# RWKV-7 chunk inverse in four groups with the transposed product merged, alternating heads, rates ahead of decays

## The chip, the cores and the metric

One core of a Trainium2 chip runs the whole program. The metric is the device time of one execution in microseconds; the kernel before takes 2446.75 us (median of 3 runs, 2444.73 to 2447.14).

## What is computed

A diffusion backbone of two layers over 256 context tokens and 256 latent tokens of width 1024. Layer 0 is a Hyena long convolution and a dense SwiGLU; layer 1 is a bidirectional RWKV-7 time mixing and a top-2-of-8 expert SwiGLU. The change touches the RWKV-7 mixer, whose recurrence the reference writes as a scan over tokens, for 16 heads of width 64 and two directions:

```python
def step(S, inp):
    r_t, w_t, k_t, v_t, a_t, b_t = inp
    sa = jnp.einsum('bhvk,bhk->bhv', S, a_t)
    S = S * w_t[:, :, None, :] + sa[..., None] * b_t[:, :, None, :] + v_t[..., None] * k_t[:, :, None, :]
    return S, jnp.einsum('bhvk,bhk->bhv', S, r_t)
```

## The kernel before, in words

**Stages.** The program is one long list of instructions for each engine, kept in order by semaphores: Hyena and the dense SwiGLU to about 784 us of the profiled span, a preparation of RWKV to 850 us, eight pairs of heads to about 1380 us, then the experts. Each pair of heads is one call of `pair(i, more)` on PE, ACT, DVE and POOL, written out eight times; SP loads the next pair's weights.

**One pair.** The 512 tokens are 8 chunks of 64, two to a block of 128 partitions, so NB = 4 blocks for each direction d, and 2 NB = 8 blocks x for each head h of the pair. Instead of a scan, each chunk is solved at once, which needs the inverse of a 64x64 unit triangular matrix for every head, direction and chunk. `scores` (L1350) makes the products of the keys; `first_join` on DVE puts the first ones into `TM`; then a hardware loop `Fori(0, LOOPED)` (L1392) of 4 levels doubles the inverted blocks inside 32x32 blocks, and `last_first` and `last_second` join the 32s to 64s. Every one of those products is a 32x32 tile, four of them in the four quarters of the array.

**One level of the loop,** with h = 0 and 1 as the two groups:
- PE `level_first(h)` (L1297): waits for `level_turned`, multiplies `AB` by `TN` (the blocks of `TM`, transposed) into bank h.
- ACT `first_copy` (L2033): copies bank h to `YP`, 128x256.
- PE `level_second(h)` (L1306): waits for `level_copied`, multiplies `YP` by `TM` into bank 2 + h.
- DVE `join` (L2791): merges the new entries from bank 2 + h into `TM` under a mask of bits, 128x256; `turn_level` (L2774) then transposes `TM` into `TN`, and only then is `level_turned` raised.

The counts that PE waits for inside the loop are registers, `lv * 2 + constant`. `settle` (L659) raises a counter that nobody in this stage waits for; it marks for the program where earlier work is done, and rides on the wait instruction before it.

**Ahead work.** While pair i is being solved, the projections of pair i + 1 are made. PE: `ahead_keys` (L1235 to 1237), `ahead_decay` (L1248, waits for ACT's copy of the keys because it uses their bank), `ahead_rate` (L1256). ACT: `ahead_rates` does the two decay sigmoids (L1992) and then the two rate sigmoids (L1996). DVE: `ahead_scan` (L2705, L2708) needs the decay sigmoids, then `ahead_rate` (L2713 to 2722), then the pair's own `m_ready` (L2831), `n_ready` (L2838), `g_ready` (L2844) and the first states (L2849). PE's `ahead_values` (L1271) may start only when `n_ready_1` is done, because it writes the bank that `n_ready` reads.

**Order of the small products.** The 64x64 products of `scores` (L1350), the third scores (L1370), and the later sums (L1441, L1452, L1463, L1473) go through one head and then the other. The program's float32 product appears as two MATMUL records and two LDWEIGHTS records.

## Time and profile before

| | us |
|---|---|
| median of 3 runs | 2446.75 (2444.73 to 2447.14) |
| the profiled execution, its own time | 2449.69 |
| its span | 2447.9 |
| PE busy | 2349.8 (96%), 24762 matmuls |
| DVE busy | 1600.3 (65%) |
| ACT busy | 1267.7 (52%) |
| granted TensorE clock, mean | 0.982 of full |
| the eight pairs of heads, about 850 to 1380 us | 530 |

How it is read: the slices of the page show PE nearly full everywhere, but busy time of overlapping small matmuls says little about how close they follow each other. So the pairs are read from the order of time: the starts of groups of records on one engine, the idle time ahead of them, and what ended it. "issue" is idle time for which the profile has no releaser.

### The profile page before, as it was taken

Reading aid. Unit: us, or ns where it says so; the run is one execution under the profiler, and the core shown is the slowest. Engines: PE = TensorE matmul, PEld = TensorE weight load, DVE = VectorE, ACT = ScalarE, POOL = GpSimd, SP = SyncE. Lnnn points to the kernel's source line nnn. Section 1 sums busy time; section 2 is a strip of 40 time slices with the busy share of each in tenths; the row PEclk is TensorE's granted clock in tenths of the full one; section 3 lists DMA queues with packets and bytes.
Section 4 is the critical chain, followed back from the end, with each engine's and each line's share of the span. In section 5 each row is a group of like instructions: output and inputs, shape, how many; then the busy total and the mean of one; then the engine's idle time right before and its main releaser. Section 6 shows DMA issues by size and latency. Waiting matters only on the chain.

```text
span 2447.9 us, 57064 instructions
## 1 busy us (share of the span) xinstructions
PE 2349.8 (96%) x24762; PEld 1909.6 (78%) x24762; DVE 1600.3 (65%) x1808; ACT 1267.7 (52%) x1400; POOL 233.4 (10%) x212
## 2 busy tenths in 40 slices
PE   8999999999999899889988989999999999999998
PEld 4677676888886477777776778888888888888887
DVE  2544876222324946555565378888888888888887
ACT  4322025222222844444444277777777777777774
POOL 2000642000000332211111100000000000000000
PEclk8999999999999899999999999999999999999999
DMA  7566126332324201111111479999999999999993
GB/s 268 188 224 241 52 87 172 86 103 86 103 86 142 80 21 32 32 31 32 31 32 44 146 272 368 334 369 333 370 335 369 336 366 337 365 339 361 344 362 134
DMA packets 249079, 490.41 MB, mean 200 GB/s; under 512 B 14615, under 2 KB 107567, under 8 KB 248623
## 3 DMA queue, kind: packets, MB, share of 16 engines
q1 hardware_dynamic: 247214, 481.31, 55.5%
q10 hardware_dynamic: 1730, 7.10, 0.8%
q8 instruction: 109, 1.79, 0.3%
q14 instruction: 26, 0.21, 0.0%
HBM read 486.29 MB, written 2.10 MB: 200 GB/s over the span
## 4 chain that ended last, share of the span: by engine, by line
PE 92%; DVE 3%; issue 2%; ACT 1%; DMA 1%; SPq 0%; POOL 0%; DVEq 0%; ACTq 0%
PE bank L1621 26%; PE bank L1648 12%; PE bank L1157 3%; PE bank L1158 3%; PE bank L1159 3%; PE bank L1271 2%; PE bank L1297 2%; PE bank L1034 2%; PE bank L1063 2%; PE bank L1035 2%; PE bank L1036 2%; PE bank L1175 2%; PE bank L1174 2%; PE bank L1176 2%; PE bank L1306 1%
## 5 line engine op out<-in xcount | busy, mean ns | idle before, releaser
L2966 DVE TENSOR_TENSOR w_low<-expert_w,w_high 128x1792 fp32r<-128x1792 f32 (+2 forms) x384 | 769.0, 2023 | 125.3 <-ACT w_high L2165 123.7
L2165 ACT CAST w_high<-expert_w 128x1792 fp32r<-128x1792 f32 (+2 forms) x384 | 652.9, 1701 | 247.0 <-PE bank L1621 154.3
L1621 PE MATMUL bank<-w_high,xg_high 128*128 128x448 f32 x1024 | 294.2, 369 | 4.0 <-DVE xg_low L2956 4.0
L1621 PE MATMUL bank<-w_low,xg_high 128*128 128x448 f32 x1024 | 291.7, 366 | 0.0
L1621 PE MATMUL bank<-w_high,xg_low 128*128 128x448 f32 x1024 | 291.5, 366 | 0.0
L1621 PEld LDWEIGHTS bank<-w_high,xg_high 128*128 128x128 f32 x1024 | 191.3, 189 | 20.1 <-DVE xg_low L2956 4.1
L1621 PEld LDWEIGHTS bank<-w_low,xg_high 128*128 128x128 f32 x1024 | 193.2, 189 | 15.5
L1621 PEld LDWEIGHTS bank<-w_high,xg_low 128*128 128x128 f32 x1024 | 192.9, 188 | 15.4
L1648 PE MATMUL bank<-w_high,hid_high 128*128 128x512 f32 x448 | 175.3, 391 | 0.0
L1648 PE MATMUL bank<-w_high,hid_low 128*128 128x512 f32 x448 | 174.5, 389 | 0.0
L1648 PE MATMUL bank<-w_low,hid_high 128*128 128x512 f32 x448 | 174.3, 389 | 0.0
L1157 PE MATMUL bank<-u_high,ring_high 128*128 128x512 f32 x352 | 139.2, 395 | 2.1 <-DVE u_low L2616 1.6
L1158 PE MATMUL bank<-u_low,ring_high 128*128 128x512 f32 x352 | 138.9, 395 | 0.0
L1159 PE MATMUL bank<-u_high,ring_low 128*128 128x512 f32 x352 | 138.4, 393 | 0.0
L2635 DVE TENSOR_TENSOR arena<-arena,bank 128x512 f32 (+1 forms) x22 | 15.1, 687 | 127.5 <-ACT arena L1927 127.5
L1648 PEld LDWEIGHTS bank<-w_high,hid_low 128*128 128x128 f32 x448 | 84.1, 188 | 17.8
L1648 PEld LDWEIGHTS bank<-w_low,hid_high 128*128 128x128 f32 x448 | 84.1, 188 | 16.7
L1648 PEld LDWEIGHTS bank<-w_high,hid_high 128*128 128x128 f32 x448 | 84.1, 188 | 16.6
L1927 ACT ACTIVATE arena<-bank 128x512 f32<-128x512 f32 x22 | 13.2, 598 | 158.9 <-PE bank L1159 158.9
L2791 DVE COPY_PREDICATED arena<-arena,bank 128x256 f32<-128x256 int32 x64 | 27.5, 430 | 84.8 <-PE bank L1306 84.8
L1157 PEld LDWEIGHTS bank<-u_high,ring_high 128*128 128x128 f32 x352 | 66.5, 189 | 18.2 <-issue 3.0
L2033 ACT COPY arena<-bank 128x256 f32<-128x256 f32 x80 | 29.4, 383 | 96.8 <-PE bank L1297 96.4
(426 smaller groups left out, 4200.5 us busy)
## 6 DMA issues: line engine op xcount, KB each, us to landing
expert_w<-in_moe_w_dram SPq DMA_DIRECT2D x192, 1792.0 KB, 9.4
arena<-in_mod_w_dram SPq DMA_DIRECT2D x48, 1024.0 KB, 8.1
arena<-in_ffn_w_dram SPq DMA_DIRECT2D x44, 512.0 KB, 5.2
arena<-in_hy_w_in_dram SPq DMA_DIRECT2D x12, 1024.0 KB, 5.2
arena<-in_rw_w_rkv_dram SPq DMA_DIRECT2D x48, 256.0 KB, 2.8
arena<-in_ffn_w_dram SPq DMA_DIRECT2D x11, 1024.0 KB, 4.9
arena<-in_hy_w_out_dram SPq DMA_DIRECT2D x4, 1024.0 KB, 9.2
arena<-in_rw_w_out_dram SPq DMA_DIRECT2D x8, 512.0 KB, 3.4
```

The lines of the kernel that those rows point to most:

```text
L1034: pe.matmul(bank[m % 4][:, :], wh[:, k, :], uh, start=(k == 0), stop=False)
L1035: pe.matmul(bank[m % 4][:, :], wh[:, k, :], ul, start=False, stop=False)
L1036: last = pe.matmul(bank[m % 4][:, :], wl[:, k, :], uh, start=False, stop=(k == KT - 1))
L1063: last = pe.matmul(bank[2 * part + f][:, :], fwd[:, tt, (2 * part + f) * P:(2 * part + f + 1) * P], ZT[:, 2 * s + tt, half * 512:half * 51 ...
L1157: pe.matmul(bank[b + h][:, :], wh[:, c, :], uh, start=(k == 0), stop=False)
L1158: pe.matmul(bank[b + h][:, :], wh[:, c, :], ul, start=False, stop=False)
L1159: last = pe.matmul(bank[b + h][:, :], wl[:, c, :], uh, start=False, stop=(k == KT - 1))
L1174: pe.matmul(bank[m][:, :], wh[:, o, :], hh, start=first, stop=False)
L1621: last = pe.matmul(bank[b0 + v][:, 0:EH], x[:, k, :], w_[:, kk, v * EH:v * EH + EH], start=(k == 0 and x is XGH and w_ is wh), stop=(k == ...
L1648: last = pe.matmul(bank[4 + half][:, :], x[:, f, :], w_[:, f - 4 * i_, :], start=(c == 0 and f == 0 and x is HTH and w_ is wh), stop=(c == ...
L2165: act.copy(high_piece(kind, n), piece(kind, ering[q % ERN], n // 2, n % 2))\
L2966: dve.tensor_tensor(piece(kind, low[s], n // 2, n % 2), piece(kind, ering[s], n // 2, n % 2), high_piece(kind, n).bitcast(F32), ALU.subtract)\
```

## The change

- **Four groups.** The levels run over (h, d), one head in one direction, 4 blocks each. Both products of a group go to the same bank, 2h + d. ACT's copies and DVE's joins become 128x128 and twice as many.
- **Merged transposed.** `level_second` swaps its operands, so that it gives the transposed product; `join` merges it straight into `TN` (the bits of the masks are stored the other way round), and raises `level_ready`. Behind the four joins `turn_back` transposes `TN` into `TM` and raises `level_turned`.
- **Waits in the loop.** `level_first` waits for `level_ready`. `level_second` waits for `level_turned` and `level_copied`, whose counts now differ (READY is 20 a pair, COPIED 18).
- **Rates ahead of decays** on PE and ACT; DVE's order stays.
- **Heads alternate** in the 64x64 products; the sums at L1441 wait for the last copy of both heads at once.
- In the dense stage, a semaphore `u_whole` on DVE is replaced by the chain on which the next chained instruction waits.

```diff
-PER_PAIR = 2 * (LOOPED + 1)
+GROUPS = 4
+READY = GROUPS * (LOOPED + 1)
+COPIED = GROUPS * LOOPED + 2
+PRODUCTS = 2 * COPIED
 LD_KEYS, LD_LORA, LD_VALUES, LD_QUERIES, LD_PAIR = 32, 64, 96, 128, 160
 
 
...
-                          [near(b, a) for b in LEVELS for a in (True, False)] +
+                          [near(b, a) for b in LEVELS for a in (False, True)] +
                           [level(C // 2, False), level(C // 2, True)], 1)
     return (common.astype(np.float32), layer0.astype(np.float32), layer1.astype(np.float32),
...
-            return 2 * PER_PAIR * i + 4 * lv + 2 * half + h + 1
+            return PRODUCTS * i + 2 * GROUPS * lv + (GROUPS if lv < LOOPED else 2) * half + h + 1
 
         CHUNKS = [[0, 1, 2, 3, 4, 5, 6, 7], [3, 2, 1, 0, 7, 6, 5, 4]]
...
             def ahead_rate(j):
                 if isinstance(j, int) and j == 0:
                     pe.wait_ge(sem("gap_turned"), 2)
+                pe.wait_ge(sem("ld_pair"), j * LD_PAIR + LD_LORA)
                 step(pe, "pair_copies", "z_copy_1", j - 1)
                 for d in range(2):
...
 
-            def level_first(h, count):
-                pe.wait_ge(sem("level_turned"), count)
+            def level_first(h, d, ready):
+                pe.wait_ge(sem("level_ready"), ready)
                 settle(pe)
-                for x in range(2 * NB):
+                for x in range(d * NB, d * NB + NB):
                     for j in range(4):
                         q, cs = slice(HC * j, HC * j + HC), slice(HC * (j % 2), HC * (j % 2) + HC)
-                        last = mm(bank[h][q, x * HC:x * HC + HC], AB[h][q, x, cs], TN[h][q, x, :], start=True, stop=True)
+                        last = mm(bank[2 * h + d][q, x * HC:x * HC + HC], AB[h][q, x, cs], TN[h][q, x, :], start=True, stop=True)
                 last.then_inc(sem("level_products"), 1)
 
-            def level_second(h, count):
-                pe.wait_ge(sem("level_copied"), count)
+            def level_second(h, d, turned, copied):
+                pe.wait_ge(sem("level_turned"), turned)
+                pe.wait_ge(sem("level_copied"), copied)
                 settle(pe)
-                for x in range(2 * NB):
+                for x in range(d * NB, d * NB + NB):
                     for j in range(4):
                         q = slice(HC * j, HC * j + HC)
-                        last = mm(bank[2 + h][q, x * HC:x * HC + HC], YP[h][q, x, :], TM[h][q, x, :], start=True, stop=True)
+                        last = mm(bank[2 * h + d][q, x * HC:x * HC + HC], TM[h][q, x, :], YP[h][q, x, :], start=True, stop=True)
                 last.then_inc(sem("level_products"), 1)
 
             def last_first(h, i):
-                pe.wait_ge(sem("level_turned"), PER_PAIR * i + 2 * LOOPED + h + 1)
+                pe.wait_ge(sem("level_ready"), READY * i + GROUPS * LOOPED + 2 * h + 2)
                 settle(pe)
...
                 def scores(name, b0, left, right):
-                    for h in range(2):
-                        r = hd(h)
-                        for x in range(2 * NB):
-                            d, b = divmod(x, NB)
-                            for s_ in range(2):
-                                t = slice(b * P + s_ * C, b * P + s_ * C + C)
-                                last = mm(bank[b0 + h][hd(s_), x * C:x * C + C], left[d][r, t], right[d][r, t],
+                    for x in range(2 * NB):
+                        d, b = divmod(x, NB)
+                        for s_ in range(2):
+                            t = slice(b * P + s_ * C, b * P + s_ * C + C)
+                            for h in range(2):
+                                last = mm(bank[b0 + h][hd(s_), x * C:x * C + C], left[d][hd(h), t], right[d][hd(h), t],
                                           start=True, stop=True)
-                        last.then_inc(sem("pair_products"), one("pair_products", f"{name}_{h}"))
+                                if x == 2 * NB - 1 and s_ == 1:
+                                    last.then_inc(sem("pair_products"), one("pair_products", f"{name}_{h}"))
 
...
                     for h in range(2):
-                        level_first(h, lv * 2 + (PER_PAIR * i + h + 1))
+                        for d in range(2):
+                            level_first(h, d, lv * GROUPS + (READY * i + 2 * h + d + 1))
                     for h in range(2):
-                        level_second(h, lv * 2 + (PER_PAIR * i + h + 1))
+                        for d in range(2):
+                            level_second(h, d, lv * GROUPS + (READY * i + 2 * h + d + 1),
+                                         lv * GROUPS + (COPIED * i + 2 * h + d + 1))
                 step(pe, "pair_vectors", "out_masked_1", i)
                 for d in range(2):
...
                     .then_inc(sem("pair_products"), one("pair_products", "bonus_sum"))
                 if more:
                     ahead_keys(i + 1, range(KT))
+                    ahead_rate(i + 1)
                     ahead_decay(i + 1)
-                    ahead_rate(i + 1)
 
...
                     ahead_key_sum(i + 1)
-                for h in range(2):
-                    step(pe, "pair_copies", f"wu_copy_{h}1", i)
-                    settle(pe)
-                    for x in range(2 * NB):
-                        d, b = divmod(x, NB)
+                step(pe, "pair_copies", "wu_copy_11", i)
+                settle(pe)
+                for x in range(2 * NB):
+                    d, b = divmod(x, NB)
+                    for h in range(2):
                         for s_ in range(2):
                             last = mm(bank[4 + s_][hd(h), x * C:x * C + C], Q[hd(s_), 2 * h + d, b, 0:C],
                                       Btok[d][hd(s_), b, hd(h)], start=True, stop=True)
                 last.then_inc(sem("pair_products"), one("pair_products", "m_sum"))
...
                 for d in range(2):
+                    step(act, "ahead_products", f"rate_{d}", j)
+                    act.activation(AS[d], bank[6 + d][:, :], ACT.Sigmoid, bias=dcol("rw_a0", j + 8 * d))\
+                        .then_inc(sem("ahead_copies"), one("ahead_copies", f"rate_sig_{d}"))
+                for d in range(2):
                     step(act, "ahead_products", f"decay_{d}", j)
                     act.activation(SG[d], bank[4 + d][:, :], ACT.Sigmoid, bias=dcol("rw_w0", j + 8 * d))\
                         .then_inc(sem("ahead_copies"), one("ahead_copies", f"decay_sig_{d}"))
-                for d in range(2):
-                    step(act, "ahead_products", f"rate_{d}", j)
-                    act.activation(AS[d], bank[6 + d][:, :], ACT.Sigmoid, bias=dcol("rw_a0", j + 8 * d))\
-                        .then_inc(sem("ahead_copies"), one("ahead_copies", f"rate_sig_{d}"))
 
             def ahead_key_log(j):
...
 
-                def first_copy(lv, h):
-                    act.wait_ge(sem("level_products"), level_product(i, lv, 0, h))
-                    act.copy(YP[h].rearrange("p x c -> p (x c)"), bank[h][:, 0:2 * NB * HC]).then_inc(sem("level_copied"), 1)
+                def first_copy(lv, h, d):
+                    act.wait_ge(sem("level_products"), level_product(i, lv, 0, 2 * h + d))
+                    act.copy(YP[h][:, d * NB:d * NB + NB, :].rearrange("p x c -> p (x c)"), bank[2 * h + d][:, d * P:d * P + P])\
+                        .then_inc(sem("level_copied"), 1)
+
+                def last_copy(h):
+                    act.wait_ge(sem("level_products"), level_product(i, LOOPED, 0, h))
+                    act.copy(YP[h].rearrange("p x c -> p (x c)"), bank[2 * h][:, 0:2 * NB * HC]).then_inc(sem("level_copied"), 1)
 
                 def z_copy(h):
...
                                              per_stream(fold_shift[0], k, 1), ALU.mult, ALU.add)
-                last.then_inc(sem("u_whole"), 1)
+                link(last)
 
             def u_low(j):
                 dve.wait_ge(sem("u_high"), j + 1)
-                dve.wait_ge(sem("u_whole"), j + 1)
                 g, c = j // 2, 2 * (j % 2)
                 dve.tensor_tensor(UL[g][:, c:c + 2, :], UT[:, 2 * j:2 * j + 2, :], UH[g][:, c:c + 2, :].bitcast(F32),
...
 
-                def turn_level(h):
-                    dve.transpose(TN[h].rearrange("p b c -> p (b c)"), TM[h].rearrange("p b c -> p (b c)"))\
-                        .then_inc(sem("level_turned"), 1)
-
                 def first_join(h):
...
+                    dve.sem_inc(sem("level_turned"), 2)
+
+                def join(lv, h, d):
+                    dve.wait_ge(sem("level_products"), level_product(i, lv - 1, 1, 2 * h + d))
                     settle(dve)
-                    dve.copy_predicated(by_dir(TM[h], HC), each_block(level_bits[lv - 1]),
-                                        by_dir(bank[2 + h][:, 0:2 * NB * HC], HC))\
-                        .then_inc(sem("pair_vectors"), one("pair_vectors", f"joined_{lv}_{h}"))
-                    step(dve, "pair_vectors", f"joined_{lv}_{h}", i)
-                    turn_level(h)
+                    mask = level_bits[lv - 1][:, d, :].unsqueeze(1).to_broadcast([P, NB, HC])
+                    dve.copy_predicated(TN[h][:, d * NB:d * NB + NB, :], mask,
+                                        bank[2 * h + d][:, d * P:d * P + P].rearrange("p (b c) -> p b c", c=HC))\
+                        .then_inc(sem("level_ready"), 1)
+
+                def turn_back(lv, h, d):
+                    dve.wait_ge(sem("level_ready"), READY * i + GROUPS * lv + 2 * h + d + 1)
+                    part = slice(d * NB, d * NB + NB)
+                    dve.transpose(TM[h][:, part, :].rearrange("p b c -> p (b c)"), TN[h][:, part, :].rearrange("p b c -> p (b c)"))\
+                        .then_inc(sem("level_turned"), 1)
 
                 for h in range(2):
                     first_join(h)
@@ -2807,7 +2822,11 @@
                 dve.tensor_copy(DC, DCn).then_inc(sem("pair_vectors"), one("pair_vectors", "chunk_decay"))
                 for lv in range(1, LOOPED + 1):
                     for h in range(2):
-                        join(lv, h)
+                        for d in range(2):
+                            join(lv, h, d)
+                    for h in range(2):
+                        for d in range(2):
+                            turn_back(lv, h, d)
                 if i:
                     finish(i - 1)
...
```

## Rows read from the trace of the kernel before

**Rows 1.** windows: one pair each, then a stretch of a second level

```profile
core 0: us, PE busy (x) PEld busy (x) DVE busy (x) ACT busy (x) POOL busy (x), PEclk, DMA share, GB/s
986.24:1052.34 66.10, 59.79 (x1945) 47.25 (x1944) 37.92 (x76) 30.02 (x56) 12.59 (x12) 0.97 0.10 29
1253.00:1322.70 69.70, 60.88 (x1946) 47.55 (x1946) 38.20 (x76) 29.85 (x56) 12.57 (x12) 0.95 0.10 28
...
997.60:999.40 1.80, 1.72 (x126) 1.75 (x130) 0.70 (x2) 0.37 (x1) 0.00 (x0) 0.50 0.19 54
```

**Rows 2.** timeline of PE, loop of the third pair

```profile
start us, us, engine line op out<-in xcount [idle before <-releaser]
997.68 1.96 PE L1297 MATMUL bank<-arena 32*32 32x32 f32 x128 [0.57 <-DVE arena L2774]
...
1001.73 1.55 PE L1297 MATMUL bank<-arena 32*32 32x32 f32 x128 [0.66 <-DVE arena L2774]
...
1005.11 1.55 PE L1297 MATMUL bank<-arena 32*32 32x32 f32 x128 [0.52 <-DVE arena L2774]
```

**Rows 3.** timeline of DVE, third pair

```profile
991.37 1.27 DVE L2805 TENSOR_TENSOR arena<-bank,arena 128x512 f32<-128x512 f32 x2
...
1004.04 0.45 DVE L2791 COPY_PREDICATED arena<-arena,bank 128x256 f32<-128x256 int32 x1 [1.65 <-PE bank L1306]
1004.52 0.45 DVE L2774 STREAM_TRANSPOSE arena<-arena 128x256 f32<-128x256 f32 x1
```

**Rows 4.** PE's sequencer by source line, whole trace or one stretch

```profile
engine op xcount: duration ns min/median/max, first and last start us, forms
L1292 PEldq ALU_OP  x32: 36/36/36, 861.2 to 1342.1; - x32
...
L1392 PEldq COMPARE_BRANCH  x1: 208/208/208, 1004.4 to 1004.4; - x1
...
L659 PEldq EVENT_SEMAPHORE  x1: 51/51/51, 991.6 to 991.6; - x1
```

**Rows 5.** timeline of weight loads, fourth pair, then third

```profile
1058.66 0.64 PEld L1297 LDWEIGHTS bank<-arena 32*32 32x32 f32 x64 [0.17 <-issue]
...
1059.34 0.46 PEld L1297 LDWEIGHTS bank<-arena 32*32 32x32 f32 x40
...
1005.89 0.66 PEld L1297 LDWEIGHTS bank<-arena 32*32 32x32 f32 x64
...
1006.49 0.31 PEld L1306 LDWEIGHTS bank<-arena 32*32 32x32 f32 x25
```

**Rows 6.** ACT's copies of 128x128, by source line

```profile
L2083 ACT COPY arena<-bank x16: 266/269/273, 914.3 to 1376.5; 128x128 f32<-128x128 f32 x16
```

**Rows 7.** waits of PE, 850 to 1323 us

```profile
engine line waited for: us in total, times, longest us
PE bank L1306 <- issue: 16.8, 7, 2.8
PE bank L1297 <- DVE arena L2774: 8.8, 18, 0.7
PE bank L1248 <- ACT arena L1987: 5.4, 7, 0.8
```

**Rows 8.** page, DMA queues: packets, MB, share

```profile
q8 instruction: 109, 1.79, 0.3%
```

**Rows 9.** timeline of PE, 64x64 products, third pair

```profile
986.24 3.26 PE L1350 MATMUL bank<-arena 64*64 64x64 f32 x122
...
1029.83 1.96 PE L1452 MATMUL bank<-arena 64*64 64x64 f32 x118
```

**Rows 10.** timelines of ACT, DVE and PE, ahead work in the second pair

```profile
956.87 1.27 ACT L1992 ACTIVATE arena<-bank,arena 128x512 f32<-128x512 f32 x2
958.03 1.27 ACT L1996 ACTIVATE arena<-bank,arena 128x512 f32<-128x512 f32 x2
...
957.59 1.23 DVE L2705 TENSOR_TENSOR_SCAN arena<-arena 128x512 f32<-128x512 f32 x1 [1.51 <-ACT arena L1992]
...
966.64 1.28 DVE L2838 TENSOR_TENSOR arena<-bank,arena 128x512 f32<-128x512 f32 x2
...
968.71 1.98 PE L1271 MATMUL bank<-arena 128*128 128x512 f32 x4
```

**Rows 11.** timeline of PE, start of the first pair

```profile
850.23 5.69 PE L1350 MATMUL bank<-arena 64*64 64x64 f32 x122 [2.37 <-DVE arena L2743]
```

**Rows 12.** timeline of PE, dense stage

```profile
410.32 0.76 PE L1157 MATMUL bank<-u_high,ring_high 128*128 128x512 f32 x1 [1.58 <-DVE u_low L2616]
```

More of the change, by code:

```diff
@@ L1445, in pair @@
                     d, b = divmod(x, NB)
-                    for h in range(2):
-                        for part in range(2):
+                    for part in range(2):
+                        for h in range(2):
                             for s_ in range(2):
```

59 lines of the change are left out of this document (29 added, 30 removed).

## The prediction

> **What bounds the kernel now.** I read the windows of single pairs first, then the order of time of PE inside one pair, then DVE's, then what PE's sequencer issues between matmuls, and last the waits. The windows [rows 1] show one pair with PE recorded as busy for 59.8 of 66.1 us and DVE for 37.9: PE looks full. It isn't, in the sense that matters here. In the loop of levels a 32x32 MATMUL follows the one before it at 8.7 ns, while each is drawn much longer, so "busy" says nothing of the spacing; only the starts do. In the third pair the second, third and fourth level start at 997.68, 1001.73 and 1005.11 [rows 2]. So the second costs 4.05 us and a warm one 3.38; the fourth has the same body. PE waits for DVE ahead of these levels: 18 waits of at most 0.7 us, 8.8 us in total, for L2774 [rows 7]. DVE's row shows why: the join takes 0.45, the transposition of head 0 another 0.45, and only its end at 1004.97 lets PE begin at 1005.11 [rows 3].
>
> But behind this wait stands a second bound. PE's sequencer has work of its own at the turn of the loop: a compare-and-branch of 0.208 from 1004.4, and then a register operation and a wait instruction of 0.051 [rows 4]. From the last product of a level to the first of the next I take 0.52 for these, worked out as 0.05 ahead of the branch, its 0.21, 0.05 for the register, 0.05 for the wait, and 0.16 of steps between them and to the array. So without DVE a level would still be about 3.0, not less.
>
> **Cost of a switch between groups.** This decides the sum. In the weight loads of the fourth pair, head 0 ends at 1058.66 + 0.64 = 1059.30, head 1 starts at 1059.34; between them the sequencer computes a register (ALU_OP at L1292, 36 ns, once per iteration, 32 in all) and then waits. In the third pair, where L1306 follows L1297 and the count is in a register already, 1005.89 + 0.66 = 1006.55 and the next starts at 1006.49, ahead of that end [rows 4, 5]. The difference is 0.10. With the ends drawn in, the spacing is about 0.146 with a register to compute and 0.044 with a bare wait instruction: the sequencer leads the array by too little to hide either.
>
> **Part 1, the levels.** A new warm level issues the same 256 MATMUL (8 x 32 x 8.8 ns = 2.26 us) but switches group seven times, not three. What is computed: firsts wait for `lv * 4 + (20 i + ...)`, of which one comes with the loop's own operation, so three; seconds wait for `level_turned` with the same values and for `level_copied` with `lv * 4 + (18 i + ...)`, four values more where i is 2 or above. So seven switches at 0.146 = 1.02; plus 0.52 for the turn, and 0.02: 3.82 us, against 3.38. Does DVE or ACT bind instead? DVE's eight operations on 128x128 are about 0.28 each (half of 0.45 plus a fixed part, an estimate from [rows 3]), 2.2 us, and the join of group 0 is done long before the level ends; ACT's four copies are 0.27 each [rows 6]. Both are hidden, and so the transposition is indeed off the path. So the gain of the change (no wait for L2774) is real and smaller than what PE's own sequencer adds: +0.44 for a warm level; rounded, +0.4.
>
> Third and fourth level: i = 2 to 7, 6 x 0.8 = +4.8; i = 1, where two of the four values coincide, +0.4; i = 0, where both counts are equal and shared, 0. Sum +5.2. Second level: TensorE runs there at 0.50 of its clock, so 1.2 GHz, behind the stall [rows 1], its 128 MATMUL at L1297 take 1.96 instead of 1.55 [rows 2], the array is slower than the sequencer and hides the registers, while the 0.66 wait for DVE shrinks: -0.1 x 8 = -0.8. First level: a stall of issue bounds it (part 2), which swallows the registers: 0, and +0.4 each, 3.2 in all, if it didn't.
>
> **Part 2, the stalls.** PE waits seven times for "issue" ahead of L1306, 16.8 us, at most 2.8 [rows 7]. They stand where instructions run for the first time, and PE's queue of instructions moves 109 packets of 1.79 MB, so 16 KB each [rows 8]: I read them as waits for the program. A stretch of dense short matmuls spends a piece in less time than the next needs. Two things follow. Faster 64x64 products bring little, as they run into the same wait. And the length of a pair depends on where the pieces fall: pairs 1, 4 and 7 (counting from one) are about 3 us longer, compare 66.10 and 69.70 [rows 1]. The change drops a few instructions, so it shifts the phase. I take the number of long pairs as unchanged, and +-1 of them, 2.8 us, goes into the range. The Trainium skill says of this (Runtime: NRT & Kernel Launch, Instruction fetch mechanics) that blocks of 16 KiB are fetched ahead of use and the crossing is mostly hidden. By it the stalls would be something else and would not move; the row's 2.8 us at most isn't hidden, and I keep it.
>
> **Part 3, alternating heads.** `scores` (L1350) for head 0 and then head 1 takes 3.26 us for 122 recorded of 128 MATMUL, 26 ns each; L1452, whose neighbours already differ in rows and banks, takes 1.96 for 118 of 128, 16 ns [rows 9]. If the alternated ones get this, `scored_0` comes at the end of all 64 products instead of half way, 0.15 to 0.2 later (64 x 15 ns against 32 x 26), and the start of the levels hangs on DVE behind it (the masks at L2805 start at 991.37 and end about when PE enters [rows 3]). Against it stands a fetch gain of about 0.45 in half of the pairs. Net 0, with bounds of +0.2 and -0.5 a pair. In pair 8, without ahead work, the sums alternate too: -0.4. [...]
>
> **Part 4, rates ahead of decays.** Now in the second pair ACT's decay sigmoids (1.27 each) start at 956.87, the scan at 957.59, DVE runs without a pause to `n_ready_1` at 966.64 + 1.28 = 967.92, PE's L1271 starts 0.8 later at 968.71 [rows 10]. With rates first PE doesn't meet the wait for ACT's key copy at L1248, 5.4 us in seven waits [rows 7], and goes on to `wu` 0.8 earlier. The rates' own waits are no new ones: the loads' is the one that the decays had at this place, and `z_copy_1` is over when the keys are done. But the decays' copy is no earlier, and ACT makes two rate sigmoids first: the group of decays comes as late as the group of rates does now, 956.87 to 958.03, +1.15. Scan +1.15, everything behind it on DVE +1.15, L1271 at scan + 11.68 in terms of the old scan. It was at 11.12 here (957.59 to 968.71): +0.56. Over the seven pairs the old distance was 11.38, 11.12, 11.65, 10.98, 11.11, 11.04, 12.79: +0.30, +0.56, +0.03, +0.70, +0.57, +0.64, -1.11 = +1.7. From L1271 on the pair is constant. Before pair one PE already waits 2.37 for DVE [rows 11], the same chain is 1.15 later, nothing covers it: +1.15.
>
> **Part 5, `u_whole`.** One semaphore becomes the chain; a chained wait on DVE may delay `u_low`, on which L1157 waits 1.58 once [rows 12]: +0.3, bounds 0 and +1.
>
> **Sum.** 5.2 - 0.8 + 0 - 0.4 + 1.7 + 1.15 + 0.3 = +7.15 us. The profiled execution is 2449.7, the median 2446.75, 2.9 under it; the terms are differences, so they go onto the median: 2453.9.
>
> **Rivals.**
> R1, registers are hidden: a switch costs 0.044 whether or not a value is computed. Then a level is 2.26 + 7 x 0.044 + 0.52 = 3.1, -0.28 for each of 16 warm levels, -4.5 instead of +5.2 and the rest shrinks to: 2453.9 - 9.7 = 2444. For it: the sequencer's operations are only 36 ns long. Against: the 0.10 in [rows 5]. It decides at 0.083 a switch, where 3.38 is met. 0.20.
> R2, DVE isn't the chain in the ahead zone: PE keeps its 0.77 and the scan's delay vanishes in slack: about -0.8 x 7 instead of +1.7 and 1.15 less, 2453.9 - 8.5 = 2445.4. Against: DVE's unbroken row. 0.13.
> R3, the phase of the pieces: the three long pairs become like the others, -8.4, 2445.5; or one or two become long, 2456.7 to 2459.5. 0.12, the halves alike.
> R4, slower still: `level_second`'s two waits against registers don't fit in one instruction. 0.1 more at four switches, 0.4 x 16 warm levels = +6.4: 2460.3. For it: two register values at once, which no wait of the kernel before has. Against: one wait instruction already does two things, as L659's counter rides on it [rows 4]. 0.13.
> R5, the change doesn't do what it says: heads alternate, the products stay at 26 ns, `scored_0` is 0.75 later: with a third of it absorbed 0.5 x 8 = +4, 2458. 0.05, inside the range.
> The forecast and its near variants: 0.37.
>
> **How the numbers follow.** 0.2% is 4.9 us, about what a measurement of this kernel can tell from no change: faster is below 2441.9, slower above 2451.6. The forecast lies at 2453.9 with its own range of 2449 to 2458, of which about a quarter is "same". R1, R2 and half of R3 lie near 2445, within the bound, a third of each beyond it (R1 with R2 together: 2435). Slower: 0.27 + R3 0.05 + R4 0.12 + R5 0.05 = 0.49, rounded 0.47; faster 0.20; same 0.33. The range must reach R1 to R3 below and R4 above: 2438 to 2461.
>
> **What would show it.** Warm levels in pairs 3 to 8 start 3.8 apart (3.1: R1; 4.2: R4) with seven ALU_OP per iteration; in the first pair 3.4. No wait for DVE ahead of a level. L1248 without a wait, decay sigmoids 1.15 after their old place, L1271 half a us later. Pair one starts at 851.4. Alternated L1350 under 20 ns a product. The count of "issue" waits over 2 us stays near seven. The prediction is wrong if levels start 3.1 apart, or if DVE has slack behind the scan.

## The result and the profile after

The changed kernel takes 2459.23 us (median of 5 executions, 2454.19 to 2462.30), the kernel before 2446.29 beside it: 1.0049 times, 95% interval 1.0037 to 1.0061, so +12 us (the medians are 12.9 apart) and slower by more than the 0.2% that a measurement can tell. The prediction was 2453.9 in a range of 2438 to 2461, with slower as the likeliest. The time lies inside; how far the working was right is another question, and most of what follows is about that.

The profiled execution of the changed kernel is the shortest of its five (2454.19, a span of 2452.4) and that of the kernel before (2449.69) lies 3.4 above its median, so the two traces show only 4.5 of the 12 us; the longest of the five, 2462.3, had a mean granted clock of 0.972 where the profiled one had 0.978.

I cut the seven pairs with ahead work into stages, each by the first record of a line (or, for the levels, by the branch that turns the loop), and summed each stage over the pairs. Key products are those of L1235 to 1237, value products those of L1271 (L1273 in the changed kernel). This table is worked out from the traces:

| stage, sum over pairs one to seven, us | before | after | |
|---|---|---|---|
| pair's start to the end of the first level | 88.0 | 89.9 | +1.9 |
| second to fourth level | 75.6 | 72.9 | -2.7 |
| fourth level to first key product | 47.2 | 48.8 | +1.6 |
| first key product to first value product | 140.4 | 141.6 | +1.2 |
| first value product to the pair's end | 121.3 | 125.5 | +4.2 |
| sum | 472.5 | 478.8 | +6.3 |

The first pair starts 2.0 earlier in this execution (848.26 against 850.23), and that comes from the program's first 410 us, where the two traces differ by 2.8 already; behind the seven pairs the traces differ by 0.1 more.

The levels. Timeline of PE in the third pair of the changed kernel, columns as in [rows 2], which it answers:

```profile
989.14 1.55 PE L1299 MATMUL bank<-arena 32*32 32x32 f32 x128 [2.02 <-DVE arena L2820]
...
993.59 1.94 PE L1309 MATMUL bank<-arena 32*32 32x32 f32 x115 [2.70 <-issue]
995.71 2.06 PE L1299 MATMUL bank<-arena 32*32 32x32 f32 x128 [0.18 <-DVE arena L2802]
...
999.49 1.59 PE L1299 MATMUL bank<-arena 32*32 32x32 f32 x128 [0.27 <-DVE arena L2802]
...
1002.78 1.61 PE L1299 MATMUL bank<-arena 32*32 32x32 f32 x128 [0.25 <-DVE arena L2802]
```

A warm level is 999.49 to 1002.78, 3.29 us, where the kernel before had 3.38. The waits ahead of a level have shrunk from 0.5 to 0.7 us to some 0.25, and the turn of the loop lies in them. DVE in the same level, which answers [rows 3]:

```profile
1001.59 1.42 DVE L2802 COPY_PREDICATED arena<-arena,bank 128x128 f32<-128x128 int32 x4 [1.11 <-PE bank L1309]
1002.92 0.88 DVE L2809 STREAM_TRANSPOSE arena<-arena 128x128 f32<-128x128 f32 x4
```

The four transpositions start at 1002.92, when PE is in the next level, and end at 1003.80, ahead of its first second product at 1004.28. They are off the path, as the prediction had it. What PE's sequencer computes, by source line, second products and first ones of the fourth level (answers [rows 4]):

```profile
L1304 PEldq ALU_OP  x4: 32/32/32, 1004.1 to 1005.2; - x4
...
L1294 PEldq ALU_OP  x3: 32/32/36, 1003.0 to 1003.7; - x3
```

Seven register operations a level, as worked out. So the mechanism was there, and its price was not.

The ahead work. Timelines of DVE, PE and ACT in the third pair of the changed kernel, which answer [rows 10]:

```profile
1022.06 1.22 DVE L2717 TENSOR_TENSOR_SCAN arena<-arena 128x512 f32<-128x512 f32 x1 [2.67 <-ACT arena L2003]
...
1031.12 1.28 DVE L2857 TENSOR_TENSOR arena<-bank,arena 128x512 f32<-128x512 f32 x2
...
1029.31 1.15 PE L1480 MATMUL bank<-arena 64*64 64x64 f32 x62
1032.55 3.50 PE L1273 MATMUL bank<-arena 128*128 128x512 f32 x4 [2.09 <-DVE arena L2857]
1035.97 0.45 PE L1501 MATMUL bank<-arena 64*64 64x64 f32 x8
...
1021.34 1.27 ACT L2003 ACTIVATE arena<-bank,arena 128x512 f32<-128x512 f32 x2
```

PE has finished its sums at 1030.5 and waits 2.09 us for `n_ready_1` (1031.12 + 1.28 = 1032.40). Then four matmuls take 3.50 us, which took 1.98 in the kernel before. The windows of the changed kernel say why (stretch, then engines, then the granted clock, columns as in [rows 1]):

```profile
1032.55:1035.97 3.42, 3.42 (x4) 1.14 (x4) 2.05 (x6) 0.00 (x0) 1.23 (x1) 0.55 0.00 0
```

The clock is at 0.55 of full on average, so for most of the stretch at 1.2 GHz, behind a wait of 2.09 us, and full again from 1036 on. In the kernel before no value product was at half clock (1.2 GHz). In the trace of the changed kernel there are three such places, behind the waits of pairs three, six and seven (2.09, 1.89 and 2.23 us), and the half clock in the eight pairs sums to 85 us instead of 51. The length of the wait alone doesn't decide it: pairs one and two waited 1.93 and 2.18, and their value products ran at the full clock. The waits of PE over the seven pairs (line, waited for, us in total, times, longest):

```profile
PE bank L1309 <- issue: 15.4, 7, 2.9
PE bank L1273 <- DVE arena L2857: 12.2, 7, 2.2
PE bank L1299 <- DVE arena L2820: 9.5, 6, 2.0
PE bank L1299 <- issue: 7.6, 7, 2.4
...
PE bank L1299 <- DVE arena L2802: 3.6, 15, 0.3
```

The wait of the levels for DVE fell from 8.8 to 3.6, that at L1248 (5.4) is gone, and a new one of 12.2 us stands ahead of the value products. This is the row that I would look at first in such a comparison: the wait was not taken away, it was moved, and it grew. The row of L2820 is new as well: faster scores bring PE to the first level earlier, and there it waits for the masks that DVE makes. Without the alternation (below) that row is gone.

### The profile page after: what moved, and what is told of

Its sections match the earlier page's. It is cut to its first block, busy times and chain, and to the rows that moved or that the text cites. A ratio compares the mean times of both kernels' runs of the same rounds, so it can differ in the third digit from the quotient of the medians.

```text
span 2452.4 us, 57640 instructions
## 1 busy us (share of the span) xinstructions
PE 2332.3 (95%) x24762; PEld 1892.1 (77%) x24762; DVE 1611.6 (66%) x1936; ACT 1275.8 (52%) x1464; POOL 233.7 (10%) x212
## 4 chain that ended last, share of the span: by engine, by line
PE 87%; DVE 8%; issue 2%; ACT 2%; DMA 1%; SPq 0%; POOL 0%; DVEq 0%; ACTq 0%
PE bank L1628 25%; PE bank L1655 12%; PE bank L1159 3%; PE bank L1160 3%; PE bank L1161 3%; PE bank L1273 2%; PE bank L1299 2%; PE bank L1065 2%; PE bank L1036 2%; PE bank L1037 2%; PE bank L1038 2%; PE bank L1177 2%; PE bank L1176 2%; PE bank L1178 2%; PE bank L1309 1%
## 5 line engine op out<-in xcount | busy, mean ns | idle before, releaser
L2802 DVE COPY_PREDICATED arena<-arena,bank 128x128 f32<-128x128 int32 x128 | 37.8, 300 | 79.9 <-PE bank L1309 74.8
L2040 ACT COPY arena<-bank 128x128 f32<-128x128 f32 x128 | 34.1, 266 | 100.2 <-PE bank L1299 95.0
L1273 PE MATMUL bank<-arena 128*128 128x512 f32 x128 | 70.3, 660 | 12.2 <-DVE arena L2857 12.2
```

The source lines that it names most:

```text
L1273: last = mm(bank[6][:, :], wst[:, 2, k, :], XV[:, k, :], start=(k == 0), stop=(k == KT - 1))
```

## Experiments

Each is compared with runs of the kernel before on the same chip; "+x" is worked out from the ratio. Where a run is set against the changed kernel's median, the two come from different occasions, and the kernel before read 2446.29 beside the changed one and 2447.81 to 2449.02 beside the others; the difference by the two ratios is the fairer one and stands with it.

**The parts alone and taken back.** First the levels alone: the kernel before with the four groups, the merged transposed product and `u_whole` replaced, so of the change all but the order of rates and decays and that of the heads. On PE:

```diff
                     for h in range(2):
-                        level_first(h, lv * 2 + (PER_PAIR * i + h + 1))
+                        for d in range(2):
+                            level_first(h, d, lv * GROUPS + (READY * i + 2 * h + d + 1))
...
```

> The kernel before with the four groups, the merged transposed product and u_whole's replacement alone; the order of rates and decays and of the heads stays as before. By the price of a switch in the prediction (0.146 us with a register) a warm level would cost 3.8 us and the kernel about 4 us more than before. By the price read from the changed kernel (0.07 to 0.09 with a register) a warm level costs 3.1 in the first two pairs and 3.3 in the others against 3.4 to 3.5, so the levels behind the first give 3 us in all; with the first levels' waits for the program, which may move either way by 3 us, the time is 2440 to 2447. In the ahead zone the wait at the decays stays and L1271 doesn't wait 1 us or more for DVE, and no stretch behind it is at half the clock.

Measured: 2450.33 us, 1.0001 (0.9988 to 1.0014). A fourth level costs 3.3 from the third pair on and 3.0 to 3.2 in the first two. Second to fourth level give 1.9 us over the seven pairs; the stage from the pair's start to the end of the first level takes 2.0 of it back. From first key product to first value product it is 141.0 (before 140.4), and no value product is at half clock. The levels alone are neither a gain nor a loss.

Then the changed kernel with the decays first:

```diff
                     ahead_keys(i + 1, range(KT))
-                    ahead_rate(i + 1)
                     ahead_decay(i + 1)
+                    ahead_rate(i + 1)
```

and the same on ACT.

> The changed kernel with the decays ahead of the rates again on PE and ACT. Theory A (the order of rates and decays costs most): the scan starts 1.15 us earlier, from the first key product to the first value product 19.1 us instead of 20.24 in each of seven pairs (-8.0), the half clock behind L1271 is gone (-4), and the first pair starts 1.15 earlier: 10 to 13 us less than the changed kernel. Rival B (the first levels and their waits for the program cost it): the time stays within 4 us of the changed kernel.

Measured: 2446.42 us, 0.9989 (0.9973 to 1.0005), 13 us less than the changed kernel's median and 15 by the ratios. The key-to-value distance is 137.9 over seven pairs against 141.6: 19.06 to 19.39 in five of the pairs (19.1 was expected in all), 20.71 and 21.08 in two that wait for issue on the way. PE in the third pair, to be laid beside the changed kernel's rows above:

```profile
1032.09 1.15 PE L1480 MATMUL bank<-arena 64*64 64x64 f32 x62
1033.16 1.98 PE L1273 MATMUL bank<-arena 128*128 128x512 f32 x4
1035.08 0.45 PE L1501 MATMUL bank<-arena 64*64 64x64 f32 x8
```

No wait, and 1.98 for the four products again. DVE's scan is at 1022.36 there and its `n_ready` at 1031.41 ends at 1032.69, still ahead of PE. From value product to the pair's end it is 120.9 instead of 125.5. So of the 13 us some 3.7 are the distance, 4.6 the clock behind it, both seen in this trace; 1.6 belong to the first pair, where the wait ahead of L1353 fell from 4.0 to 2.4 us; the rest isn't seen in single traces, since executions of one kernel differ by more than that.

The rates first alone, on the kernel before:

```diff
                     ahead_keys(i + 1, range(KT))
+                    ahead_rate(i + 1)
                     ahead_decay(i + 1)
-                    ahead_rate(i + 1)
```

> The kernel before with the rates ahead of the decays on PE and ACT, and nothing else. If this order is the cause, it shows without the rest of the change: the distance from the first key product to the first value product is 20.24 us in each of seven pairs instead of 19.57 to 21.58 (+1.3 in sum), the first pair starts 1.15 later against the dense stage, and some of the value products and what stands behind them run at the half clock (+3 to 5): 5 to 7 us more than the kernel before. The prediction's own step gave +2.9 (1.7 and 1.15) without the clock. If the cause needs the levels too, within 2 us of the kernel before.

Measured: 2450.92, 1.0020 (1.0008 to 1.0032), +4.9 us. The distance is 20.22 in six pairs and 21.75 in one, 143.1 in all (+2.7). The wait is there, but shorter than in the changed kernel: L1271 for DVE 6.5 us in 6 times, at most 1.4. And value product to the pair's end is 121.1, as before: no half clock, where 3 to 5 us of it had been expected; the profiled execution is the third shortest of the ten, and the longer ones can't be seen. The distance and the first pair's wait (2.37 to 3.98) make 4.3 of the 4.9. So the order costs about 5 us by itself, 13 to 15 inside the changed kernel. It doesn't just add up.

The alternation alone, on the kernel before (in each of the 64x64 products `for h in range(2)` moves inward, as in the diff of the change):

> The kernel before with the alternating heads alone. The products at L1452 take 0.98 instead of 1.52 until the next group, 0.5 a pair, those at L1473 0.1 less; where the value products wait for DVE anyway (pairs 2, 5 and 7) this is worth nothing. The start of the levels is 0.1 to 0.15 later in each pair. Sum -2 to 0 us, and up to 3 either way from the first levels' waits for the program.

Measured: 2447.92, 0.9999 (0.9987 to 1.0010). Where the prediction had two numbers for the sums, the trace has 0.98 instead of 1.52 from the first record of L1441 to that of L1452, in each of the seven pairs. The key-to-value distance fell by 3.2 over the seven pairs; the median shows none of it.

What lets the clock fall, then? The changed kernel without the alternation:

```diff
-                    for x in range(2 * NB):
-                        d, b = divmod(x, NB)
-                        for s_ in range(2):
-                            t = slice(b * P + s_ * C, b * P + s_ * C + C)
-                            for h in range(2):
+                    for h in range(2):
+                        r = hd(h)
+                        for x in range(2 * NB):
+                            d, b = divmod(x, NB)
+                            for s_ in range(2):
...
```

and the same in the third scores and in the four later sums.

> The changed kernel without the alternating heads: levels, rates first and u_whole's replacement. Theory: behind the rates the value products wait for DVE, so all that alternation gives the later sums (0.54 at L1459, 0.12 at L1480 a pair) only lengthens that wait, and a wait of over 2 us in its sum with the stalls ahead of it is what lets the clock fall. Then without alternation the distance from the first key product to the first value product is 20.24 as in the changed kernel, the value products run at the full clock, and the time is 4 to 6 us less than the changed kernel: 2453 to 2455, 1.003 of the kernel before. Rival: the clock falls by the levels and the rates alone, then the half clock stays behind L1271 and the time is within 2 us of the changed kernel.

Measured: 2453.53, 1.0020 (1.0011 to 1.0030), 5.7 us less than the changed kernel's median, inside the expected 4 to 6, and 7 by the ratios. The distance is 20.22 to 20.31 in all seven pairs, so DVE still sets it. But PE comes later to the wait:

```profile
1035.07 1.95 PE L1273 MATMUL bank<-arena 128*128 128x512 f32 x4 [1.26 <-DVE arena L2857]
```

The wait is 1.26 in the third pair, not 2.09, and the products run at the full clock. Over the pairs the wait sums to 6.4 us instead of 12.2. One pair in seven (the second, 3.58 until the first state product instead of 1.88) was at half clock all the same, against three. So the alternation, worth nothing ahead of a wait for DVE, lengthened it, and where it did the clock fell more often. Three places in one trace and one in another are a small count, so here are the value products behind whose start half clock stood within 4 us, in all fourteen traces; each such place is worth 1.6 us or more:

| kernels | traces | at half clock, of the places |
|---|---|---|
| rates first and alternating heads (the changed one, equal counts, 64 more, one more at each switch) | 4 | 12 of 28 |
| rates first, one head and then the other | 2 | 1 of 14 |
| decays first, later sums alternating | 6 | 2 of 42 |
| decays first, one head and then the other | 2 | 0 of 14 |

The two together do it, then, and either alone hardly ever. In the first row the waits for DVE ahead of the places at half clock and of those at full clock overlap (1.57 to 2.23 us, with one of no such wait behind a stall of 1.85 for issue, and 0 to 2.18). The two of the third row stand behind stalls of 1.91 and 2.00 for issue just ahead of the value products.

**What a group switch costs.** Equal counts, so that both waits of a second product use one register:

```diff
-COPIED = GROUPS * LOOPED + 2
-PRODUCTS = 2 * COPIED
+COPIED = READY
+PRODUCTS = 2 * (GROUPS * LOOPED + 2)
...
-                    act.copy(YP[h]..., bank[2 * h]...).then_inc(sem("level_copied"), 1)
+                    act.copy(YP[h]..., bank[2 * h]...).then_inc(sem("level_copied"), 2)
...
```

> The changed kernel with the count of copies made equal to that of the turned blocks (20 a pair, the two last copies count double), so that both waits of a second product take one register and four ALU operations of a level are gone, in all pairs as now in the first. If a register costs about 0.055 us at a switch, the third and fourth level of pairs three to eight shorten from 3.28 to 3.06: -2.6 us, and the levels of the second pair are as now. If the prediction's 0.10 held, -4.8 us. If the sequencer hides it, 0. The places of the program's pieces move by some 20 instructions in all, which can add or take 3 us at a first level.

Measured: 2454.35, 1.0023 (1.0011 to 1.0034), 4.9 less than the changed kernel's median and 6 by the ratios. Third and fourth level of pairs three to seven fell from 3.28 to 3.12 on average, and the single level shown here to 3.10; levels two to four of the seven pairs from 72.9 to 70.6. In the first pair, where the changed kernel has no such registers either, the fourth level is as it was (3.06 and 3.07). A level of the sixth pair, and the start of the next:

```profile
1208.65 1.55 PE L1299 MATMUL bank<-arena 32*32 32x32 f32 x127 [0.28 <-DVE arena L2802]
...
1210.03 1.39 PE L1309 MATMUL bank<-arena 32*32 32x32 f32 x127
1211.75 0.42 PE L1299 MATMUL bank<-arena 32*32 32x32 f32 x29 [0.33 <-DVE arena L2802]
```

Four registers cost 0.16 to 0.19 of a level, so 0.04 to 0.05 each, half of the prediction's 0.10. The levels account for 2.3 of the 4.9 us; the rest is open.

The other way round, one more instruction at each switch:

```diff
                 pe.wait_ge(sem("level_ready"), ready)
                 settle(pe)
+                settle(pe)
```

and the same in `level_second`.

> The changed kernel with one more instruction (the counter that nobody waits for) at each of the eight group switches of a level. It measures what one instruction of PE's sequencer costs there. If the sequencer leads the array by too little to hide it, as the prediction took, each costs 0.05 to 0.15 and a warm level goes from 3.29 to between 3.7 and 4.5, at 0.05 to 0.15 a switch. If the lead hides it, the level stays at 3.3. In the first pair 3.06 to 3.11 goes up by the same amount.

Measured: 2488.38, 1.0148 (1.0128 to 1.0168), +36 us. A level from the fourth pair's trace:

```profile
1088.16 2.18 PE L1300 MATMUL bank<-arena 32*32 32x32 f32 x128 [0.26 <-DVE arena L2804]
1090.23 2.06 PE L1311 MATMUL bank<-arena 32*32 32x32 f32 x128
1092.66 1.93 PE L1300 MATMUL bank<-arena 32*32 32x32 f32 x128 [0.37 <-DVE arena L2804]
```

4.50 us instead of 3.29: 1.2 over eight switches, 0.15 for each instruction. The sequencer's time is on the path, and so are the registers by the run above: R1's condition (a value costs nothing) doesn't hold, and yet the level is no slower than before. Both can only be true if the rest of the level is cheaper than I had it.

**Where the first level's length comes from.** 64 more instructions for PE ahead of the first pair:

```diff
+                if i == 0:
+                    for _ in range(64):
+                        settle(pe)
                 step(pe, "ahead_vectors", "a_1", i)
```

> The changed kernel with 64 more instructions for PE (the counter that nobody waits for) where PE waits 4 us for DVE ahead of the first pair. They themselves are hidden there. If the waits for issue in the first levels are waits for the program, whose places depend on where 16 KB pieces begin, then the first level's length changes from pair to pair: those of pairs 1, 4, 6 and 8 (7.3, 8.7, 8.3 and 7.1 us now) and of the others (5.4 to 6.1) swap in part, by 2 us or more in at least three pairs, while all other stages stay within 0.3. If the stalls have another cause, each first level keeps its length within 0.5.

Measured: 2463.35, 1.0052 (1.0031 to 1.0073). They were not hidden: by source line they stand from 846.4 to 856.0,

```profile
L661 PEldq EVENT_SEMAPHORE  x64: 51/51/51, 846.4 to 856.0; - x64
```

0.152 us apart, three times their own 51 ns, and the first pair began at 856.30. So its total says little, but its stages do. The time from entering the levels to the end of the first was 7.3, 5.7, 6.1, 8.7, 5.4, 8.3, 5.5, 7.1 for the eight pairs of the changed kernel and 5.6, 6.0, 7.9, 5.7, 6.0, 8.7, 5.4, 7.8 here. Pair four lost 3.0, and pairs one and three moved by 1.7 and 1.8: by the bound of 2 us that is one pair where I had expected three. But nothing else in these pairs is different in the code, so the place of the instructions does it, with a smaller swing than I had expected. Chance from one execution to the next is no rival for the large moves: the kernel before and the one with the rates first alone, which have the same number of instructions, have 4.7, 5.7, 4.8, 7.7, 5.9, 5.3, 7.1, 4.8 and 5.2, 5.1, 5.1, 7.8, 5.9, 5.3, 6.8, 4.6, within 0.6 of each other; the changed kernel and the one with the decays first, as long but with that code in another order, are within 1.1. So the 3.0 is well clear of it, the 1.7 and 1.8 less so.

Two more shifts, with tiny products at the program's start, on the best version below:

```diff
             wake(6)
+            for _ in range(16):
+                pe.matmul(bank[7][0:HC, 0:HC], silu_zero[0:HC, 0:HC], silu_zero[0:HC, 0:HC], start=True, stop=True)
```

> The kernel with decays first, equal counts and scores by head, with 16 tiny float products (64 instructions of PE) at the program's start, where PE waits for the inputs. If the first levels' waits for the program depend on where the 16 KB pieces begin, which pairs have the long first level (over 7.4 us now in pairs 4 and 6, over 6.2 in 2, 7 and 8) changes, by 2 us or more in two pairs at least. The sum of the first levels (52.3) may go to anything between 47 and 57, and the time by as much. If it doesn't matter where the pieces begin, each stays within 0.5.

> The same with 32 tiny products, 128 instructions, half a piece. The place of the long first levels moves on once more. The sum of the first levels 47 to 57; the best of the three shifts would be the version to carry on, 2440 to 2450.

Measured: 2449.68, 0.9996 (0.9987 to 1.0006), and 2446.92, 0.9996 (0.9987 to 1.0005). Without a shift the long ones (7.9 and 8.9) were pairs four and six, with 64 they are three, six and eight (7.7, 8.0, 8.6), with 128 two and five (8.7, 8.2). They move with the code's place, by more than 2 us in several pairs, and in sum (from entering the levels, over eight pairs) they stay: 52.3, 51.9, 52.0. No shift was worth its instructions.

**Better versions.** Decays first and equal counts:

> The changed kernel with the decays first and with the equal counts, so both edits together. If they add up: the levels behind the first 2.9 us less than with the decays first alone, 2443.5; no value product at the half clock. If what the levels give is taken back at the value products, which wait for DVE, 0 in the pairs in which the levels end earlier but DVE's chain behind them, too, starts by them: then the gain stays. Expected 2443 to 2444, 0.2% under the kernel before.

Measured: 2444.58, 0.9987 (0.9974 to 1.0000): 3 us under the kernel before, where 0.2% had been expected.

The same with the three scores through one head and then the other:

> As the one with decays first and equal counts, but the three scores go through one head and then the other, as in the kernel before; the later sums still alternate. The start of the levels is set by DVE behind the first score of head 0: 5.91 instead of 6.07 from the start of a pair, -0.15 a pair, -1.2 us. Rival: the alternation gives room for the program's pieces, then the first levels are longer by 0.3 or more each and the time is 1 to 3 us more.

Measured: 2444.55, 0.9986 (0.9977 to 0.9996), the only one whose interval lies below 1, though by less than the 0.2% that a measurement can tell; against the run above it is no different. The levels did not start 0.15 earlier, as expected: 5.96 to 6.40 from the start of pairs two to eight, 5.97 to 6.09 in the run above. Of the change it keeps the four groups and the alternating sums. It is 3 us under the kernel before and 15 under the changed one.

## Why the prediction was right, and where it wasn't

**The levels: the term with the wrong sign.** I had +5.2 and -0.8, the trace has -2.7 over seven pairs. The count was right: seven registers, and no instruction more for the second wait, since the trace has the wait for `level_turned` on the register operation and that for `level_copied` on the counter instruction. So R4 is out. The prices were wrong, all to one side. The starts of all MATMUL of the level from 999.49 to 1002.78, worked out from the trace beside the forecast's terms, in us:

| | forecast | measured |
|---|---|---|
| steps inside the eight groups | 2.26 | 2.14 |
| seven steps over a switch | 1.02 | 0.72 |
| turn of the loop | 0.54 | 0.44 |
| level | 3.82 | 3.30 |

R1's dividing point, 0.083 a switch, did not divide: the switches came out on the forecast's side of it and the level on R1's side of 3.38. The second level went as forecast in kind, -0.6 over eight pairs for -0.8: where a MATMUL follows at 13.4 ns, at half clock, the switches are mostly 0.00 to 0.04. In the first pair, where no second product needs a register of its own, the level is 3.06, where the forecast had 3.4 and R1 3.1.

**The first level and the phase: the right mechanism, sized at nothing.** I had 0 with a bound of 2.8 for one more long pair. Measured +1.9 over seven pairs in these two traces, and +4.2 over all eight: in the kernel before two of pairs two to eight have a first level that ends more than 12.9 us behind the pair's start, in the changed kernel three. That is R3 on its slow side, one long pair more. Over all kernels, the time to the end of the first level summed over eight pairs is 98.2 to 98.7 in the three with the old levels (before, rates alone, heads alone) and 102.5 to 105.7 in the ten with the new ones whose levels have no added instruction, wherever the code lay. So the new levels cost some 5 us in the first level, which takes back what the later three give. A shift doesn't cure it. Why three and not two is open: the pair is a few instructions shorter, a level's body some longer, and I have no run that separates them. The Trainium skill (Runtime: NRT & Kernel Launch, Instruction fetch mechanics) has such crossings mostly hidden; here waits of up to 2.9 us move when 64 instructions are added, so by the runs they depend on the code's place, as waits for the program would, and are not hidden. That they are fetches is inferred.

**Rates ahead of decays: right in the mean, and short by the clock.** The step that the prediction worked out in most detail held to a few hundredths in six pairs and to 0.24 in the last: L1271 waits for the end of an unbroken chain on DVE, +0.30, +0.56, +0.03, +0.70, +0.57, +0.64, -1.11 forecast, and +0.25, +0.53, 0.00, +0.66, +0.53, +0.60, -1.35 measured; +1.2 in place of +1.7. Ahead of the first pair the wait grew from 2.37 to 3.98, 1.6 of the forecast 1.15, and in the run with the decays first it was 2.4 again. R2 is out: DVE has no slack behind the scan. What I did not have is that "PE waits for DVE ahead of L1271" costs a second time. The wait came to 1.6 to 2.2 us in six of seven pairs, and behind three of them stood half clock, +4.2 in this trace. In the typical execution it may be 5 to 7, if all that the run without alternation gave back is clock; that is an estimate. [rows 1] and [rows 2] held the warning, a second level at half clock behind a stall, and I used it only for the levels.

**Alternating heads: right alone, wrong in company.** 16 ns a product was right (L1353 takes 2.10 for 128 where it had 3.26 for 122 recorded), R5 is out. The later start of the levels was +0.08 to +0.2 in five of pairs two to eight and -0.4 and -0.5 in the other two, net near 0 as forecast; with the heads alternating alone the levels start up to 0.3 earlier in six of them, so the 0.15 to 0.2 isn't the alternation's. But I had the sums' gain only in pair eight, and left out that in the other seven it comes to stand ahead of a wait for DVE, where it is worth nothing with the rates first (and costs clock) and something with the decays first. The sum of the parts measured alone is +4.9 us (0, 4.9 and 0); the whole is +12. The other 7 us are this meeting (the intervals of the four ratios together leave it 1 to 13), and the run without alternation, 7 us under the changed kernel by the ratios, says the same.

**`u_whole`:** it has no run of its own, and +0.3 is inside the noise of a median. But the wait that the forecast named, ahead of L1157, is 1.51 to 1.58 us in the three traces with the semaphore and 1.78 to 1.93 in nine of the eleven with the chain (1.54 and 1.59 in the other two): the +0.3 is there.

So the total came out inside the range, 5 us above the forecast, by errors that partly cancelled: -7 to -8 in the levels, +4 in the first levels, +4 to +5 for the clock, and the rest in what the medians show and single traces don't. That the sum of them fell within the range is luck. The chance of 0.47 for slower was fair, but the forecast's main reason, registers in PE's sequencer, cost some 0.3 us a level and did not make the levels slower, and the first reason of the slowdown was the part that had +2.9 in the sum.

## What to carry to other kernels

An engine that is made faster ahead of a wait for another engine has gained nothing and may lose clock by it: add up, for each change, how long the wait behind it becomes, and look whether such stalls are followed by half clock elsewhere in the same trace. Prices for short runs of instructions are to be read from short runs. And where a change has several parts, their measured sum should be compared with the whole: here one part in the wrong order turned a kernel that can't be told from the one before (0.9989) into one 0.5% slower.

## What the runs showed of the hardware

- Counter instructions of PE's sequencer with nothing between them follow at 0.152 us, though each is recorded as 51 ns; in a loop of short products one more at each of eight switches costs 0.15 in the mean. A register operation there costs 0.04 to 0.05.
- At the full clock a run of 32 MATMUL of 32x32 goes at 8.5 ns, a run of 64 at 8.8 (8.2 in its first half, 9.4 in its second); at half clock 13.4, and there the steps over a switch are mostly 0.00 to 0.04 us.
- Products of 64x64 go at 26 ns one head after the other and at 16 with the heads alternating.
- Behind a wait of 2.09 us four products of 512 columns took 3.50 us at 0.55 of the clock; without a wait 1.98, and behind one of 1.26 they took 1.95, though one of seven such places in that kernel was at half clock too, behind a wait of 1.21. Two waits of 1.93 and 2.18 were followed by the full clock: the wait's length alone doesn't tell.
